# Forgetting softmax of block one: a step's weight group is issued behind its transposes and value products

## What is computed

```python
c = jnp.cumsum(jnp.transpose(log_f, (0, 2, 1)), axis=-1)
for blk in range(seq // C_BLOCK):
    q0 = blk * C_BLOCK; q1 = q0 + C_BLOCK
    s = jnp.einsum('bhqd,bhkd->bhqk', qh[:, :, q0:q1], kh[:, :, :q1]).astype(jnp.float32) * scale
    s = s + c[:, :, q0:q1, None] - c[:, :, None, :q1]
    s = jnp.where(mask[None, None], s, -jnp.inf)
    p = jax.nn.softmax(s, axis=-1)
    outs.append(jnp.einsum('bhqk,bhkd->bhqd', p.astype(vh.dtype), vh[:, :, :q1]))
```

## Time and profile before

| | us |
|---|---|
| Median of 3 runs | 2579.55 (2578.6 to 2582.15) |
| Profiled execution, its own time | 2576.96 |
| Its span, first to last instruction | 2575.2 |
| PE busy | 2540.1 (99%) |
| DVE busy | 1474.6 (57%) |
| ACT busy | 1098.3 (43%) |
| Mean granted TensorE clock | 0.999 |
| The forgetting softmax, S(0) to the end of G(35) | 195.7 to 278.3 |

### The profile page before, as it was taken

The page is one execution under the profiler, slowest core; times in us unless marked ns, Lnnn a source line. Parts: engine busy times, 40 slices in busy tenths (PEclk is TensorE's granted clock), DMA queues, the critical chain, the costliest instruction groups (busy, mean ns, idle before and its releaser), DMA issues.

```text
span 2575.2 us, 33170 instructions
## 1 busy us (share of the span) xinstructions
PE 2540.1 (99%) x12770; PEld 2116.3 (82%) x12770; DVE 1474.6 (57%) x2786; ACT 1098.3 (43%) x1929; POOL 35.2 (1%) x70
## 2 busy tenths in 40 slices
PE   8999999999999999999999999999999999999998
PEld 6888878888888887888888787888888887888887
DVE  6766668554546678644444686544447586444445
ACT  3436455333644556332222344335636483422223
POOL 0000000000000000000000000001000000000000
PEclk9999999999999999999999999999999999999999
DMA  4320223123313221233333231223132222333332
GB/s 147 90 66 30 79 59 102 50 82 96 93 58 95 81 90 57 70 111 98 99 99 97 76 99 58 66 90 115 44 98 69 97 72 78 94 98 98 94 95 89
DMA packets 118172, 217.54 MB, mean 84 GB/s; under 512 B 14080, under 2 KB 21552, under 8 KB 118016
## 3 DMA queue, kind: packets, MB, share of 16 engines
q1 hardware_dynamic: 114096, 201.60, 25.2%
q0 software_dynamic: 3776, 13.57, 2.0%
q10 hardware_dynamic: 144, 0.26, 0.0%
HBM read 211.20 MB, written 4.19 MB: 84 GB/s over the span
## 4 chain that ended last, share of the span: by engine, by line
PE 93%; DVE 4%; ACT 2%; issue 1%; DMA 0%; SPq 0%; ACTq 0%; DVEq 0%
PE bank L611 52%; PE bank L608 25%; PE bank L765 5%; PE bank L754 2%; PE bank L734 2%; PE bank L735 2%; PE bank L802 1%; PE bank L819 1%; PE bank L856 1%; PE bank L654 1%; DVE wL L1551 1%; DVE hL L1658 0%; PE bank L794 0%; DMA wraw<-in_w_in_dram 0%; ACT wH L1013 0%
## 5 line engine op out<-in xcount | busy, mean ns | idle before, releaser
L1551 DVE TENSOR_TENSOR wL<-wraw,wH 128x1024 fp32r<-128x1024 f32 (+1 forms) x388 | 460.0, 1186 | 645.3 <-ACT wH L1013 643.0
L1013 ACT ACTIVATE wH<-wraw 128x1024 fp32r<-128x1024 f32 (+1 forms) x388 | 398.2, 1026 | 887.5 <-PE bank L611 537.9
L611 PE MATMUL bank<-hH,wH 128*128 128x512 f32 x1720 | 691.1, 402 | 2.0 <-DVE wL L1551 1.0
L611 PE MATMUL bank<-hL,wH 128*128 128x512 f32 x1720 | 672.2, 391 | 0.0
L611 PE MATMUL bank<-hH,wL 128*128 128x512 f32 x1720 | 671.8, 391 | 0.0
L611 PEld LDWEIGHTS bank<-hH,wH 128*128 128x128 f32 x1720 | 323.3, 188 | 74.2 <-issue 5.1
L611 PEld LDWEIGHTS bank<-hL,wH 128*128 128x128 f32 x1720 | 323.5, 188 | 70.5 <-issue 3.8
L611 PEld LDWEIGHTS bank<-hH,wL 128*128 128x128 f32 x1720 | 323.1, 188 | 69.1
L608 PE MATMUL bank<-wH,hH 128*128 128x512 f32 (+1 forms) x736 | 282.4, 384 | 0.7 <-DVE wL L1551 0.7
L608 PE MATMUL bank<-wH,hL 128*128 128x512 f32 (+1 forms) x736 | 277.1, 376 | 0.0
L608 PE MATMUL bank<-wL,hH 128*128 128x512 f32 (+1 forms) x736 | 276.9, 376 | 0.0
(11 more groups left out here) (334 smaller groups left out, 3150.0 us busy)
## 6 DMA issues: line engine op xcount, KB each, us to landing
wraw<-in_w_in_dram SPq DMA_DIRECT2D x180, 512.0 KB, 3.5
wraw<-in_w_ffn_down_dram SPq DMA_DIRECT2D x44, 512.0 KB, 3.5
wraw<-in_w_ffn_gate_dram SPq DMA_DIRECT2D x40, 512.0 KB, 3.6
wraw<-in_w_ffn_up_dram SPq DMA_DIRECT2D x40, 512.0 KB, 3.5
wraw<-in_w_out_dram SPq DMA_DIRECT2D x24, 512.0 KB, 3.5
wraw<-in_w_up_a_dram SPq DMA_DIRECT2D x8, 512.0 KB, 3.6
wraw<-in_w_up_b_dram SPq DMA_DIRECT2D x8, 512.0 KB, 3.6
wraw<-in_w_up_c_dram SPq DMA_DIRECT2D x8, 512.0 KB, 3.5
```

The costliest lines, as they stand in the source:

```text
L611: mm = pe.matmul(bank[b.bank0 + t][:, :], w_part[:, kk, t * P:(t + 1) * P], act_part[:, k, :], start=first, stop=last)
L1013: A(wH[:, u % W_SLOTS, 0:width], wraw[:, u % RAW_SLOTS, 0:width], ACT.Copy).then_inc(S["w_hi"], 1)
L1551: V.tensor_tensor(wL[:, u % W_SLOTS, 0:width], wraw[:, u % RAW_SLOTS, 0:width], wH[:, u % W_SLOTS, 0:width].bitcast(F32), ALU.subtract).th ...
```

## The change

In the forgetting softmax alone, and on PE alone, the weight group of a step is issued at the end of the step: S(s), T(s-2), V(s-3), G(s) instead of S(s), G(s), T(s-2), V(s-3). The other softmax stages keep their order. Nothing is added or removed, and ACT's and DVE's lists stay as they are.

```diff
@@ -740,7 +740,7 @@
                         mm.then_inc(S["sc_done"], 1)
-                    if s < len(side) and side[s]:
+                    if kind != "fox" and s < len(side) and side[s]:
                         group(*side[s])
                     if 2 <= s < len(items) + 2 and weighs(items[s - 2]):
                         it, y = items[s - 2], nth_y[s - 2]
@@ -766,6 +766,8 @@
                                            start=c == 0, stop=c == nk - 1)
                         mm.then_inc(S["pv_done"], 1)
+                    if kind == "fox" and s < len(side) and side[s]:
+                        group(*side[s])
```

## The result

Over 22 runs of each kernel on the same chips the median went from 2578.06 us to 2582.2 us. The ratio is 1.0017, with a 95% interval of 1.0010 to 1.0023, so some 4.4 us slower (2.6 to 5.9); the two medians are 4.1 us apart. The 22 runs put the kernel before 1.5 us under the median of three that the prediction had started from. The profiled execution took 2583.46 us, its span is 2581.7.

A forecast was written before the change was run, and what follows sets the result against it. PE, busy 99% of the span, was taken to bound the kernel. Net waits per step summed to +3.4 us, which added to a median of 2579.55 gave 2583.0 us, range 2578.0 to 2588.0.

The forecast's parts named there:

- rival 4: Longer wait at step 18 halves PE's clock: 2584.7 us for one fall, 2586.4 for two; chance 0.06.
- The bound and the prize: PE is busy 99% of the span; only the stage's 7.5 us of stall, 0.29%, could be won.
- The chain S(s), max, exp, copy(s-2), T(s-1), with one group less of cover: T(s-1) hangs on S(s) through copy behind exp; 2.2 us long after 512 keys, 1.9 after 256.
- The other chains keep theirs.: Claimed y(s-4) still has one group, one S and one T of cover; S(s) waits for exp(s-2), two steps away.
- The walk through the timeline: Both orders followed step by step through the engines' queues; net of waits already present, +3.4 us.
- Step 14: copy(11) behind exp(13): T(12) waits 0.7, V(11) 0.4, against 0.3 before; +0.8 us.
- Step 34: V(31) waits for y(30) behind a weight split: about 1.3 us against 0.7 to 0.85; +0.4 us.
- Rival 3: No absorption in steps 18 to 32: all 5.5 us plus step 14's 0.8 are paid, 2585.8 us; chance 0.12.
- Rival 2: Faster: transposes and values come a group earlier; 2575.8 us if half of 7.5 us went; chance 0.07.
- Rival 1: Nothing to see, within 1.5 us: ACT and DVE set the AZ half's pace; 2579.5 us, chance 0.25.
- What would show it: T's waits for copies rise from 2.3 to 5 to 7 us; S(31) some 2 us later, G(35) some 3.
- three signs of being wrong: Copies start ahead of their step's exp; waits for y grow instead; the clock leaves 1.00 in steps 4 to 35.

The follow-up runs named there:

- e1: Changed kernel with ACT's copy(s-2) issued ahead of exp(s) in this softmax; ratio to the kernel before 1.0001.
- e8: Changed kernel with copy(s-2) ahead of exp(s), plus six unread products on PE ahead of T(16) in step 18; ratio to the kernel before 1.0001.
- e9: Changed kernel with each group halved, first half ahead of the transposes, second half behind the values; ratio to the kernel before 1.0000.
- e2: Changed order only from step 16 on (groups of 256 columns), old order in steps 0 to 15; ratio to the kernel before 1.0010.
- e3: Changed order only in steps 0 to 15 (groups of 512 columns), old order from step 16; ratio to the kernel before 1.0000.
- e5: Changed kernel plus twelve unread products of 256 columns on PE between S(18) and T(16); 2580.7 us, ratio to the kernel before 1.0010.
- e6: Changed kernel with the eight steps without a group moved from 1, 5, ..., 29 to 2, 6, ..., 30; ratio to the kernel before 1.0028.
- e4: Changed kernel with step 18 alone put back to the old order; 2581.0 us, ratio to the kernel before 1.0010.

## Why the prediction held, and where it did not

**The number.** The forecast of +3.4 us lies in the measured interval of 2.6 to 5.9, by a chain that was right and a clock that was left out. That the absolute 2583.0 is so near the measured 2582.2 is luck: the median of before that it started from was 1.5 us too high, and the clock's 1.2 to 1.9 us were missing from the sum. By ratio the measured 1.0017 lies between the forecast (1.0013) and rival 4 (1.0020).

**The bound and the prize.** Held: PE's own work is the same, and behind the stage the profile differs by 0.3 us.

**The chain S(s), max, exp, copy(s-2), T(s-1), with one group less of cover.** Held, and shown by e1 and e8 (the copy moved) and e9 (half the cover); e2 with e3 agree. Its length was to be 2.2 us behind 512 keys and is 2.26 at step 32. Step by step, with waits counted from the usual distance to the row ahead, forecast then measured in the changed kernel: step 6 0.15, 0.14; step 18 1.8, 1.73; step 22 0.5, 0.53; step 24 0.65, 0.67; step 26 0.4, 0.54; step 27 0.9, 1.02; step 30 0.2 and 0.5, 0.21 and 0.45; step 32 1.05, 1.03. Step 20 is hidden in that profile by the slow clock; at full clock, in e5, T(18) waits 246.45 - 246.07 - 0.07 = 0.31 and V(17) 247.01 - 246.45 - 0.33 = 0.23, together what the kernel before has there, where 0.1 less was forecast.

**"The other chains keep theirs."** This sentence was wrong for V's wait for y. It counts the cover from V(s-4) to y(s-4), but y(s-4) also stands in DVE's list behind max(s-1), which hangs on S(s-1), and that cover lost the group as well. The walk through the timeline had the effect at steps 14 and 30 (0.4 and 0.5 us) without naming it, so the sum hardly suffered. The 1.0 us that e8 leaves lies mostly in such waits, by its list of waits, and the expectation of e6 failed by them.

**The terms that were off.** Step 14: T(12) 0.7 and V(11) 0.4 forecast, 0.42 and 0.53 measured. Step 34: V(31) was to wait 1.3 and waited 0.85, as before, since the weight split ahead of y(30) had moved with it. Together they take 0.6 us from the +3.4, and the small excess at steps 26 and 27 gives 0.3 back; the waits alone came to 3.0 to 3.1 us in the stage (e4, e5).

**The clock.** This is where the weights were wrong. Rival 4 had 0.06 and needed one fall at step 18; that is what the profile shows. That it happened in many runs is inferred from the means (0.9964, against 0.9974 in e4 and 0.9979 in e5, which differ from it in step 18 alone); the runs without a profile don't say where their clock fell. The argument against it, that the 1.2 us wait of before had not lowered the clock in one profile, was one sample. The prediction also calls the end of the mixer before sparse, while PE is marked busy throughout in the earlier trace rows; low busy time is not what went ahead of that fall. The price (1.7 us a fall) was right: the profiled execution lost 84.6 - 82.8 = 1.8 us by it, and the runs on average 1.2 (e4) to 1.9 us. The forecast without it was 3.4, the measured change 4.4.

**Rival 3** (no absorption, +6.3) did not come: ACT's and DVE's backlogs did take up steps 16 to 20: from S(16) to S(20) e5, at full clock, takes 11.40 us and the kernel before 11.35. **Rival 2** fell with the copies, which start behind exp in the changed kernel too. **Rival 1** (within 1.5 us) is excluded by the interval, which begins at 2.6.

**What would show it.** T's waits for copies rose to 4.8 us in 7, where 5 to 7 in about eight was written, and y's stayed at 1.8, where it was 2 to 3. S(31) came 4.1 us later, counted from S(0), instead of 2, and the end of G(35) 4.7 instead of 3. The excess is the clock: in e5, where it held, they came 2.5 and 3.1 later, counted from S(2). That the clock leaves 1.00 in steps 4 to 35 was one of the three signs of being wrong that the prediction named, and it did.

## What to carry to other kernels

Count cover per chain, not per step. When work is moved within a step, list each operation that waits for another engine, follow that engine's own list back to what it stands behind, and add up what PE does in between in the old and in the new order. The moved block covers the chain whose source is ahead of it and whose consumer is behind it; here the exponential in front of a copy made a source out of S(s) where the semaphores alone name T(s-2), and on DVE the maximum in front of y did the same. Where such a wait grows to a microsecond or two, as it did in step 18, price the clock too, and take it from the mean over many runs rather than from one profile.

## What the runs showed of the hardware

With twelve useless products of 256 columns in a wait of 1.7 us the median was 1.5 us lower (2580.7 against 2582.2, ratio intervals overlapping) and the mean granted clock 0.9979 instead of 0.9964. A fall costs time only where PE has work: in the changed kernel's profile the one in step 18 cost 1.8 us, the one at 335 us at most 0.3. The fall in step 18 is not a function of one wait: it happened with waits of 0.73 and 0.40 us in step 18 (e1) and did not with 0.81 and 1.53 us in steps 18 and 19 (e4). What exactly decides it stays open here.
